# The samples' outer products of a retention layer in two row quarters of the PE array, with their stacked rows kept twice

## The reference

```python
z = rms_norm(x) @ w_in                        # 2048 -> 7168 columns
q, k, v, g_r, a, b, g_c = split(z)            # 8 heads of 128 for q, k, v
o, S = retention(rope(q), rope(k), v, S0)     # per head, gamma_h = 1 - 2^(-5-h)
...
x = h + sigmoid(h @ w_ple_gate) * rms_norm(p @ w_ple)
```

```python
S_new = gamma * S + outer(k, v)               # 128 x 128
o     = q @ S_new
```

## Time and profile before

| | |
|---|---|
| median of 3 runs | 1194.54 us (1194.06 to 1195.91) |
| the profiled execution | 1196.74 us |
| its span, first to last instruction | 1194.9 us |
| mean granted clock of PE | 0.999 of full speed |
| PE busy | 1175.8 us (98%) |
| DVE busy | 921.7 us (77%) |
| ACT busy | 606.2 us (51%) |
| POOL busy | 83.4 us (7%) |
| L534 and L535, 16 each | 7.6 and 6.3 us busy |

### The profile page before, as it was taken

How to read it: one execution, slowest core, us unless ns; L and a number is a source line. 1 busy time by engine, 2 the same in 40 slices (tenths; PEclk the granted TensorE clock), 3 DMA queues, 4 the chain that set the end, 5 groups by cost and what they waited for, 6 DMA issues and landing times.

```text
span 1194.9 us, 25304 instructions
## 1 busy us (share of the span) xinstructions
PE 1175.8 (98%) x9804; PEld 1165.1 (98%) x9804; DVE 921.7 (77%) x1481; ACT 606.2 (51%) x917; POOL 83.4 (7%) x102
## 2 busy tenths in 40 slices
PE   6999999999999999999999999999999999999998
PEld 6999999999999999999999999999999999999998
DVE  6799899999986643588779979999999764446863
ACT  7343466555556444545444344556565564455341
POOL 0000000000000012201120000000000000121000
PEclk9999999999999999999999999999999999999999
DMA  8555755555554654424556566555555456543462
GB/s 310 173 185 204 219 200 203 191 195 190 200 188 168 247 177 176 177 87 161 196 192 218 203 188 214 197 195 195 185 219 199 162 183 240 177 161 121 151 230 80
DMA packets 43465, 225.80 MB, mean 189 GB/s; under 512 B 6400, under 2 KB 13056, under 8 KB 19584
## 3 DMA queue, kind: packets, MB, share of 16 engines
q1 hardware_dynamic: 29520, 200.14, 46.9%
q10 hardware_dynamic: 13872, 24.65, 6.4%
HBM read 210.97 MB, written 13.81 MB: 188 GB/s over the span
## 4 chain that ended last, share of the span: by engine, by line
PE 82%; DVE 7%; DMA 3%; issue 3%; ACT 3%; ACTq 1%; DVEq 0%; SPq 0%
PE accum_all L476 25%; PE accum_all L477 24%; PE accum_all L478 24%; DMA raw<-w_in 3%; DVE wlo L1090 2%; ACT whi L721 1%; DVE tmp L1166 1%; PE accum_all L568 1%; PE accum_all L569 1%; PE accum_all L570 1%; DVE c_buf L1166 1%; PE ps L543 1%; PE ps L492 1%; DMA pre<-w_in 1%; ACTq L918 1%
## 5 line engine op out<-in xcount | busy, mean ns | idle before, releaser
L476 PE MATMUL accum_all<-a_hi,whi 128*128 128x264 f32 x2048 | 586.3, 286 | 3.2 <-DVE wlo L1347 3.2
L477 PE MATMUL accum_all<-a_lo,whi 128*128 128x264 f32 x2048 | 581.1, 284 | 0.0
L478 PE MATMUL accum_all<-a_hi,wlo 128*128 128x264 f32 x2048 | 580.9, 284 | 0.0
L1090 DVE TENSOR_TENSOR wlo<-raw,whi 128x2048 fp32r<-128x2048 f32 x182 | 420.1, 2309 | 173.1 <-ACT whi L721 173.0
L721 ACT ACTIVATE whi<-raw 128x2048 fp32r<-128x2048 f32 x182 | 347.6, 1912 | 158.5 <-DMA raw<-w_in 83.9
L476 PEld LDWEIGHTS accum_all<-a_hi,whi 128*128 128x128 f32 x2048 | 386.5, 189 | 7.3 <-issue 6.6
L477 PEld LDWEIGHTS accum_all<-a_lo,whi 128*128 128x128 f32 x2048 | 386.8, 189 | 0.8
L478 PEld LDWEIGHTS accum_all<-a_hi,wlo 128*128 128x128 f32 x2048 | 384.9, 188 | 0.0
L476 PE MATMUL accum_all<-b_hi,whi 128*128 128x264 f32 x672 | 191.1, 284 | 0.0
L477 PE MATMUL accum_all<-b_lo,whi 128*128 128x264 f32 x672 | 190.4, 283 | 0.0
L478 PE MATMUL accum_all<-b_hi,wlo 128*128 128x264 f32 x672 | 190.3, 283 | 0.0
(11 more groups left out here) (213 smaller groups left out, 1213.9 us busy)
## 6 DMA issues: line engine op xcount, KB each, us to landing
raw<-w_in SPq DMA_DIRECT2D x108, 1024.0 KB, 4.8
raw<-w_out SPq DMA_DIRECT2D x32, 1024.0 KB, 4.8
raw<-w_gate SPq DMA_DIRECT2D x32, 1024.0 KB, 4.8
s_new<-s_ret ACTq DMA_DIRECT2D x16, 512.0 KB, 3.6
ss_out<-s_new ACTq DMA_DIRECT2D x16, 512.0 KB, 2.6
raw<-w_pw SPq DMA_DIRECT2D x8, 1024.0 KB, 4.8
x<-x_t SPq DMA_DIRECT2D x4, 528.0 KB, 7.7
raw<-w_in SPq DMA_DIRECT2D x8, 256.0 KB, 8.0
```

The lines of the kernel that those rows point to most:

```text
L476: pe.matmul(accum[bank][:, 0:R], w_hi[:, w:w + P], hi, start=k == 0, stop=False)
L477: pe.matmul(accum[bank][:, 0:R], w_hi[:, w:w + P], lo, start=False, stop=False)
L478: mm = pe.matmul(accum[bank][:, 0:R], w_lo[:, w:w + P], hi, start=False, stop=k == k_tiles - 1)
L1090: v.tensor_tensor(wlo[:, slot, :], raw[:, side, :], whi[:, slot, :].bitcast(F32), ALU.subtract).then_inc(s.lo_ready, 1)
```

## The change

`stack` keeps the 32 rows twice, in partitions 0 to 31 and 32 to 63. `vbd` has four blocks instead of eight: samples 0 to 3 in partitions 0 to 31 and samples 4 to 7 in partitions 32 to 63. Each of the two products contracts 32 rows, the first those of the first 32 partitions, the second those of the second. No row outside these is read, so the memsets on POOL, the semaphore `zeros_set` and ACT's wait for it are gone. ACT makes one more copy (the second `stack`). `stack` and `og` move in SBUF to the place behind the smaller `vbd`.

```diff
--- before.py
+++ after.py
@@ -217,7 +217,6 @@
         self.pool_step = nc.alloc_semaphore("pool_step")
         self.ret_rs = nc.alloc_semaphore("ret_rs")
         self.sample_out_done = nc.alloc_semaphore("sample_out_done")
-        self.zeros_set = nc.alloc_semaphore("zeros_set")
         self.og_ready = nc.alloc_semaphore("og_ready")
         self.turn_done = nc.alloc_semaphore("turn_done")
         self.rt_ready = nc.alloc_semaphore("rt_ready")
@@ -295,7 +294,9 @@
     sprod = sb("sprod", [P, CT // 2, DEC, TAPS], at=heads_at)
     cursor[0] = heads_at
 
-    vbd = sb("vbd", [P, DEC, P], F32R)
+    vbd = sb("vbd", [P, DEC // 2, P], F32R)
+    stack = sb("stack", [P, P], F32R)
+    og = sb("og", [P, 3, P])
     zs = sb("zs", [P, 2, R])
     zw = sb("zw", [P, 2, R])
     qk = sb("qk", [P, 2, R])
@@ -304,8 +305,6 @@
     krow = sb("krow", [P, 2 * P])
     pmat = sb("pmat", [P, 3 * P])
     stack_cols = sb("stack_cols", [P, 2, 4, DEC], F32R)
-    stack = sb("stack", [P, P], F32R)
-    og = sb("og", [P, 3, P])
     s_prompt = sb("s_prompt", [P, P])
     gz = sb("gz", [P, R])
     sg = sb("sg", [P, R])
@@ -315,7 +314,7 @@
     heads_end = cursor[0]
     cursor[0] = max(heads_end, sb_at["e_buf"][1])
     p_in = sb("p_in", [P, PT, R])
-    assert sb_at["sprod"][1] <= sb_at["vbd"][1]
+    assert sb_at["sprod"][1] <= sb_at["og"][1]
 
     def sm(name, at, n):
         return small[:, at:at + n]
@@ -531,8 +530,8 @@
             pe.wait_ge(s.vbd_ready, n + 1)
             pe.wait_ge(s.rt_ready, n + 1)
             blocks = vbd[:, :, :].rearrange("p b v -> p (b v)")
-            pe.matmul(ps_s0[:, :], stack[:, 0:P], blocks[:, 0:4 * P], start=True, stop=True)
-            pe.matmul(ps_s1[:, :], stack[:, 0:P], blocks[:, 4 * P:8 * P], start=True,
+            pe.matmul(ps_s0[:, :], stack[0:32, :], blocks[0:32, :], start=True, stop=True)
+            pe.matmul(ps_s1[:, :], stack[32:64, :], blocks[32:64, :], start=True,
                       stop=True).then_inc(s.values_done, 1)
 
         def ret_samples(l, h):
@@ -758,9 +757,11 @@
             nc.scalar.activation(vrow[:, :], ps_tr[:, 0:2 * P], ACT.Copy)
             nc.scalar.activation(krow[:, 0:P], ps_tr[:, 2 * P:3 * P], ACT.Copy, scale=kcol(0))
             nc.scalar.activation(krow[:, P:2 * P], ps_tr[:, 3 * P:4 * P], ACT.Copy, scale=kcol(1))
+            nc.scalar.activation(stack[32:64, :], ps_s1[0:32, 0:P], ACT.Copy)
             nc.scalar.activation(stack[0:32, :], ps_s1[0:32, 0:P], ACT.Copy).then_inc(s.rows_ready, 1)
             for b in range(DEC):
-                block_of_b = nc.scalar.activation(vbd[0:32, b, :], ps_s1[0:32, P:2 * P], ACT.Copy,
+                at = 32 * (b // 4)
+                block_of_b = nc.scalar.activation(vbd[at:at + 32, b % 4, :], ps_s1[0:32, P:2 * P], ACT.Copy,
                                                   scale=cst[0:32, K_MASK + b:K_MASK + b + 1])
             block_of_b.then_inc(s.vbd_ready, 1)
 
@@ -921,7 +922,6 @@
             act.wait_ge(s.scs_out, 16 * (l + 1))
             act.wait_ge(s.sconv_step, 5 * (l + 1))
             act.dma_start(s_new[:, :], s_ret[HEADS * l * P:(HEADS * l + 1) * P, :]).then_inc(s.state_in, 16)
-            act.wait_ge(s.zeros_set, l + 1)
             head(l, 1, True, False)
             with act.Fori(2, HEADS) as h:
                 head(l, h, True, True)
@@ -1660,9 +1660,6 @@
 
         for l in range(DEPTH):
             root(l, ST_X)
-            pool.wait_ge(s.sconv_step, 5 * (l + 1))
-            nc.gpsimd.memset(vbd[:, :, :].bitcast(F32), 0.0)
-            nc.gpsimd.memset(stack[:, :].bitcast(F32), 0.0).then_inc(s.zeros_set, 1)
             with pool.Fori(0, HEADS - 1) as h:
                 ret_root(l, h)
             root(l, ST_LN)
```

## The result

The changed kernel takes **1197.9 us**, the median of 13 runs (1196.36 to 1201.01), beside 1194.83 for 13 runs of the kernel before (1193.65 to 1197.22). The ratio is 1.0025, with a 95% interval of 1.0018 to 1.0032: slower by 3.0 us (2.2 to 3.8). The forecast was 1196.8, the range 1191.0 to 1198.8. The sign and the main term came out as argued; about a third of the loss comes from a step that the prediction had costed at nothing.

What follows compares the result with a forecast made beforehand. PE, busy 98% of the span, was taken as the bound. Its two products were to take 0.63 us a head instead of 0.47, 2.2 us more in 14 heads, added to 1194.54: 1196.8 us, range 1191.0 to 1198.8.

Steps and rivals of the forecast that it cites:

- The division: PE around the two products: splitting the array by rows makes them take 0.63 us a head against 0.47, 2.2 us in all.
- Free division: Rival for PE's two products: dividing costs nothing, 0.22 us gained in each of 14 heads, 1191.4 us; chance 0.22.
- Not side by side: Rival for PE's products: array divided but both stream one after the other, +5.3 us, 1199.9 us; chance 0.14.
- Loads in a row: Rival for PE's products: second weight load waits for the first, another 0.11 us a head, 1198.3 us; chance 0.09.
- loads under the wait: Rival for PE's products: engine waits at both ends but loads weights meanwhile, -0.7 us, 1193.8 us; chance 0.07.
- The memsets and the wait on `zeros_set`: POOL's memsets and ACT's wait for them: removing them gains nothing, as the wait ends before ACT could go on.
- The second copy of the stacked rows: One more ACT instruction a head, 0.25 us, ahead of `rows_ready` and the blocks; covered by 2.6 us, so costing nothing.
- The bound named in the text: Four ACT blocks shifted 32 partitions: even 0.25 us more each would, with the copy, use 1.25 of 2.6 us cover.
- the shift ends there: ACT's delay from the extra copy was to end at L800, where ACT waits 0.72 us for PE anyhow.
- The test that I set up for this step: PE's wait list: a wait for ACT of 0.1 us or more at L526 or L534 would mean the copy's cover is gone.
- The sum: All terms of the change together: 2.2 us slower, added to the median of 1194.54, giving 1196.8 us.
- The forecast's own range: Total time if the forecast itself holds, without the rivals: 1196.0 to 1197.6 us (0.10 to 0.22 us a head); chance 0.44.

Runs made afterwards that it cites:

- e5: The changed kernel with the two `krow` products moved between the two divided products: 1209.07 us, ratio 1.0117 to the kernel before.
- e3: The kernel before with both products on partitions 0 to 31, one after the other, without the zeros or a second copy: 1200.11 us, ratio 1.0044.
- e1: The kernel before plus ACT's second copy of the stacked rows, which nothing needs, products unchanged: 1196.12 us, ratio 1.0005.
- e4: The changed kernel with both products issued twice into the same banks: 1202.02 us, ratio 1.0057 to the kernel before.

## Why the prediction was right, and where it was not

*The division* was right in its size and in its pieces. Forecast: 0.08 in, 0.11 load, 0.23 for both streams, 0.01 of offset, 0.10 out, 0.10 for the next load, 0.63 in all and 0.98 from the last pass to the second GEMM matmul. Measured: 0.10, 0.11, 0.23, 0.00, about 0.08, 0.10, and 0.97. L543, the column groups, was the right neighbour to price row quarters by; e5 gives the same 0.63 by another way. The Trainium skill, "TensorEngine Tiling (Array Packing)", section Tiling Modes, has a change of mode drain the engine; the 0.10 us at the entry and the loads that nobody made ahead agree.

*The rivals.* Free division is out: 0.97 us and not 0.60, and e3, which only divides, costs 5 us. Not side by side is out by the 0.003 us between the starts and by e3, which is what that rival describes (1.20 us, as forecast for it). Loads in a row are out by the loads at the same 230.44, loads under the wait by the absence of any load ahead of 230.44. The transposes run at the ordinary pace although they too use 32 columns; why they don't pay was not tried.

*The memsets and the wait on `zeros_set`* gave nothing, as forecast: no wait of PE in the list answers to them.

*The step that failed* is "The second copy of the stacked rows", costed at "Nothing". Two things in it were wrong. First the size: 0.25 us by one copy's duration, where ACT's chain grew by 0.56 to the end of the blocks and by 0.68 to the rounding, because instructions whose outputs start at different partitions lose their overlap. The bound named in the text (0.25 more for each of four blocks) was large enough for it, but it was held only against PE's slack at the rows. Second the sentence "the shift ends there", at L800. ACT did catch up there, but the rounding ahead of L800 was late, DVE's `wlo` with it, and for DVE I took the slack of the new state (3.1 us) as if it were that of all its list. The consumer with none was `pmat` of the last head, which L639 waits for: it already lost 0.21 us before the change (338.20 to 338.54), in a row that I had not read. The test that I set up for this step, a wait of PE at L526 or L534 in heads 2 to 7, came out negative as I said, and was the wrong test.

*The sum.* 2.2 forecast, 2.1 + 1.0 measured. Another 0.3 us of the distance to 1196.8 is the base: the kernel before has a median of 1194.83 in 13 runs, and the forecast was added to the 1194.54 of 3. The forecast's own range (up to 1197.6) didn't reach 1197.9; the whole range held it, thanks to ends that other rivals had set.

## What to carry to other kernels

Dividing the PE array costs about 0.4 us here for one visit, in and out with the uncovered loads, however many products are inside: it pays from the point where the streams that run side by side save more than that, and two products of 512 columns save only 0.23. Put everything that uses one division in one place. And an extra instruction on an engine that is half idle is priced by following its delay to the last consumer of everything behind it on the queue, above all to places that already wait a little; what the critical engine itself takes longer in between comes off that delay.

## What was not expected of the hardware

- **ACT's overlap depends on where the output starts.** Instructions of 0.34 to 0.37 us follow each other's starts by 0.25; where the output goes to another first partition than that of the instruction ahead, by 0.355 (within the blocks), 0.37 (last block to rounding) and 0.38 (`krow` to the first copy), and a step of 0.16 becomes 0.28 (copy to copy). e1, whose blocks all lie at partition 0, keeps 2.09 us for them, and 0.25 from there to the rounding. It is the change and not the distance between input and output: the last blocks all write 32 partitions away from where they read, and are back at 0.25 from one to the next. Whether it is the output's partition alone was not tried by itself.
- **Loads inside one division are made ahead, though none is made across its edge.** In e3 the second product's load starts at 230.73, 0.11 us after the first's, and its product at 230.96; in e3 and e4 the products after the first start as soon as the stream ahead is done.
- **The load of 32 rows is not shorter by much**: 181 ns for L533, against 192 ns for the 128 rows of before.
